# The inverse of the delta rule: its constant triangle as 128x128 block-diagonal tiles, one product for two heads

## The chip, the core and the metric

The kernel is one program on one core of a Trainium2 chip. The time is that of one execution on the device, in microseconds (us), and the number compared is the median of several executions. A core has TensorE (PE in the profile; its weight loads are listed apart as PEld), VectorE (DVE), ScalarE (ACT), GpSimd (POOL) and SyncE (SP), which issues most of the DMAs.

## What is computed

The reference is one decoder block on 512 tokens of width 1024, in float32: a projection, four DeltaNet heads (128 wide) beside four causal pooling groups, an output projection, and then a mixture of 32 experts, of which each token takes 4. The change touches one step of the DeltaNet heads, the inverse of a unit lower triangle of 64x64, one for each chunk of 64 tokens and each head (8 chunks x 4 heads = 32 triangles):

```python
a_mat = jnp.where(strict, jnp.einsum('bhnid,bhnjd->bhnij', k_beta, k) * decay, 0.0)
t_mat = lax.linalg.triangular_solve(a_mat, eye, left_side=True, lower=True, unit_diagonal=True)
u = jnp.einsum('bhnij,bhnjd->bhnid', t_mat, v * beta[..., None])
w = jnp.einsum('bhnij,bhnjd->bhnid', t_mat, k_beta * jnp.exp(g)[..., None])
```

The experts stream some 384 MB of weights (32 experts of 12 MB), and everything ahead of them works on 512 tokens.

## The kernel before

**Storage.** The two heads of a pair lie one above the other: head 0 of the pair on partitions 0 to 63, head 1 on 64 to 127. So the 32 triangles are 16 columns of tiles (NC = 16), each [128, 64] with two triangles in it. They are worked on in two groups of eight columns, a = 0 and a = 1. AT holds the constant triangles, TR the inverse so far (times -1 and turned, as the algorithm has it), TM its transpose, YM the masked product. All four lie in the large tile `ring`, or in `cat`, which later hold expert weights and activations.

**The inverse.** It is built in five levels (s = 0 to 4), which double the size of the blocks already inverted. For each level and group, PE makes the product of AT with TM (`level_products(s, a)`, into PSUM bank 2 + 2a), DVE masks it into YM (`level`, line 1032), PE makes the product of YM with TR (`level_update(s, a)`), ACT copies it back with its sign changed (`keep_inverse`, line 684), and DVE turns it (`turned`, line 922). Both products go through `tiles`: for each of the 8 columns one matmul for each head of the pair, with weights of 64 rows by 64 columns and 64 moving columns. A float32 matmul of the code stands as two MATMULs and two LDWEIGHTS in the trace, so that one call of `tiles` is 32 of each. There are ten calls of `level_products` and ten of `level_update`.

**The order on PE** is written out by hand: half of an input projection (`project(m, lo, hi)`, line 1468: 4 matmuls of 128x128 weights by 512 columns, 8 in the trace), then `level_products(s, 0)` and `level_update(s - 1, 1)`; the other half, then `level_products(s, 1)` and `level_update(s, 0)`. The first call, `level_products(0, 0)`, stands alone between two halves, and so does the last update. Nine groups hold one product and one update in a row.

**Around it.** DVE builds AT (lines 1019 and 1021) and the first TR (line 1023), turns it (line 922) and goes on to `conv(8)` (line 936), the causal convolution of a projection; PE's `project(m)` waits until `conv(m - 2)` has read its bank. POOL converts biases (lines 530, 533), then waits for lines 539 to 543, which spread decays over the chunks. SP loads `w_in` in ten pieces, and one 1 MB unit of the first expert's weights into slot 0 of the ring (`load_unit(0, 0, 0)`), behind the router's weights and ahead of the wait for the first projection. Later it loads `w_out` (line 384) after `u_ps`, the count of the products that use the finished inverse. The expert loop starts at about 307 us of the profile.

Of the kernel before, what the change touches and what calls it, by code (L numbers as in the profile page):

```python
# [25 lines left out]
CH = 64  # L26
NCH = T // CH
NC = 2 * NCH
# [16 lines left out]
UNIT = 2 * D  # L45
# [8 lines left out]
def moe_block(nc, x, attn_norm_w, w_in, conv_w, a_log, dt_bias, dn_norm_w, pool_w, pool_scale, w_out,  # L54
# [3 lines left out]
    with ctx:  # L58
        def sb(name, shape, dt=F32):
            return ctx.enter_context(nc.sbuf_tensor(name, shape, dt))  # L60

        def sem(name):
            return ctx.enter_context(nc.semaphore(name))


        ring = sb("ring", [P, RING * UNIT])
        late = ring[:, EARLY * UNIT:]

        def room(at, *dims):
            n = 1  # L70
            for d in dims:
                n *= d
            flat = late[:, at:at + n]
            if len(dims) == 2:
                return flat.rearrange("p (a b) -> p a b", a=dims[0])
            if len(dims) == 3:
                return flat.rearrange("p (a b c) -> p a b c", a=dims[0], b=dims[1])
            return flat
# [8 lines left out]
        junk = room(14400, D)  # L87
        GUM, NG, BI, AT, TM, YM = [room(14336 + 1024 * i, NC, CH) for i in range(6)]
        KKD, TRv = YM, YM
        sqq = room(20480, H, T)  # L90
        VTOK = room(20480, NC, P)
        wout = room(14336, KD, D)
# [130 lines left out]
        def bank(b, a=None):  # L223
            v = ps[:, b, :]
            return v.rearrange("p (a b) -> p a b", a=a) if a else v
# [9 lines left out]
        def bc(v, n, at):  # L235
# [20 lines left out]
        dx_ok, dexp_ok, nk_ok, rt_ok, rr_ok, ktok_ok, tr0_ok, tm_ok = [sem(n) for n in (  # L256
            "dx_ok", "dexp_ok", "nk_ok", "rt_ok", "rr_ok", "ktok_ok", "tr0_ok", "tm_ok")]
        qkt_ok, sqq_ok, nq_ok, vtok_ok, y_ps, ym_ok, tr_ps, tr_ok, trkv_ok = [sem(n) for n in (
            "qkt_ok", "sqq_ok", "nq_ok", "vtok_ok", "y_ps", "ym_ok", "tr_ps", "tr_ok", "trkv_ok")]
# [22 lines left out]
        def chain(eng, s, start=0):  # L282

            n = [0]

            def link(ins):
                n[0] += 1
                ins.then_inc(s, 1)
                eng.wait_ge(s, start + n[0])
            link.n = n  # L290
            return link

        def unit_src(e, u):

            if u < NGU:
                return w_gate_up[0, bass.ds(e, 1), u * P:(u + 1) * P, :].rearrange("a p c -> (a p) c")
            c = 2 * (u - NGU)
            return w_down[0, bass.ds(e, 1), c * P:(c + 2) * P, :].rearrange("a (c p) n -> p (a c) n", c=2)

        def unit_dst(slot, u):  # L300
            v = ring[:, slot * UNIT:(slot + 1) * UNIT]
            return v if u < NGU else v.rearrange("p (c n) -> p c n", c=2)
# [21 lines left out]
        def tap_of(m):  # L324

            return m + H if m < H else (m - H if m < 2 * H else m)
# [5 lines left out]
        def group(a):  # L332
            return slice(NC // 2 * a, NC // 2 * (a + 1))
# [11 lines left out]
        def _(sp):  # L345
# [20 lines left out]
            def load_unit(e, u, slot):  # L366
                sp.dma_start(unit_dst(slot, u), unit_src(e, u)).then_inc(slot_in[slot], 16)  # L367

            load_unit(0, 0, 0)
            sp.wait_ge(proj_ps, 2)  # L370
            load_piece(3)
            sp.wait_ge(bias_ok, 1)
# [9 lines left out]
                                 bc(zeros, TOPK, 1)).then_inc(zeroed, 16)  # L382
            sp.wait_ge(u_ps, 2)
            sp.dma_start(wout[:, :, :], w_out[0].rearrange("(k p) c -> p k c", p=P)).then_inc(wout_in, 16)
            sp.wait_ge(proj_ps, 18)
            load_unit(0, 8, 8)
            sp.wait_ge(pool_mix, 4)
# [85 lines left out]
        def _(pool):  # L473
            G = nc.gpsimd
            link = chain(pool, pool_step)
# [17 lines left out]
            for c in range(2):  # L493
                r = slice(CH * c, CH * (c + 1))
# [8 lines left out]
            for q in range(Q):  # L503
                r = slice(SLOTS * q, SLOTS * (q + 1))
# [24 lines left out]
            for n in range(3):  # L529
# [4 lines left out]
                else:  # L534
                    ins.then_inc(bias_ok, 1)

            pool.wait_ge(lvl_ok, 1)
            pool.wait_ge(g_ok, 1)
            G.tensor_tensor(GUM, mask(cz, NC), colb(gt[:, 8], CH), ALU.mult).then_inc(spread_ok, 1)
# [6 lines left out]
            for g, w in enumerate(WINDOWS):  # L546
                pool.wait_ge(silu_ok, NQKV + g + 1)
                src, s, i = pbuf[:, g], 1, 0
                while s < w:
                    dst = pool_t[:, i % 2]  # L550
                    link(G.tensor_tensor(dst[:, PAD:], src[:, PAD:], src[:, PAD - s:PAD + T - s], ALU.add))
                    src, s, i = dst, 2 * s, i + 1
# [316 lines left out]
        def _(dve):  # L869
            V = nc.vector  # L870
            link = chain(dve, dve_step)
# [48 lines left out]
            def turned(a):  # L920

                V.transpose(TM[:, group(a)].rearrange("p c f -> p (c f)"),
                            TR[:, group(a)].rearrange("p c f -> p (c f)")).then_inc(tm_ok, 1)
# [6 lines left out]
            def conv(m):  # L930

                t, n = cbuf[m % 2], tap_of(m)
                dve.wait_ge(tap_ok, m + 1)
                for j in range(1, CONV):
                    at = NCV + (n_conv - j) * NQKV + n
                    ins = V.scalar_tensor_tensor(out=t[:, j:], in0=bank(m % 2)[:, 0:T - j], scalar=pcol[:, at:at + 1],
                                                 in1=t[:, j:], op0=ALU.mult, op1=ALU.add)
                    if j < n_conv:
                        link(ins)
                    else:  # L940
                        ins.then_inc(conv_ok, 1)

            dve.wait_ge(bc_in, 48)
            for hh in range(2):
                r = slice(CH * hh, CH * (hh + 1))
# [40 lines left out]
            for hh in range(2):  # L986
                r = slice(CH * hh, CH * (hh + 1))
# [36 lines left out]
            for a in range(2):  # L1024
                dve.wait_ge(tr0_ok, a + 1)
                turned(a)
            conv(8)

            def level(s, a):
# [396 lines left out]
        def _(pe):  # L1426
            mm, tr = nc.tensor.matmul, nc.tensor.transpose
            def x_transposed(b, k, to):

                return tr(bank(to)[:, b * P:(b + 1) * P], xs[:, b, k * P:(k + 1) * P], ident)  # L1430

            pe.wait_ge(const_ok, 3)
            for b in range(TB):
                pe.wait_ge(x_in[b], 16)
                for k in range(KD - 1):
                    last = x_transposed(b, k, k)
# [7 lines left out]
            for b in range(TB):  # L1444
                pe.wait_ge(xdiag_ok, b + 1)
                last = mm(bank(7)[:, b * P:(b + 1) * P], ones, xdiag[:, b, :], start=True, stop=True)
# [53 lines left out]
            def rows(hh):  # L1500
                return slice(CH * hh, CH * (hh + 1))

            def chunk_of(v, n, h):
                return v[:, h, CH * n:CH * (n + 1)]
# [20 lines left out]
            def tiles(b, lhsT, rhs, a):  # L1525

                for c in range(NC // 2):
                    for hh in range(2):
                        last = mm(bank(b, 8)[rows(hh), c], lhsT[rows(hh), NC // 2 * a + c, :], rhs(hh, NC // 2 * a + c),  # L1529
                                  start=True, stop=True)  # L1530
                return last

            def of(v):
                return lambda hh, c: v[rows(hh), c, :]

            def level_products(s, a):

                pe.wait_ge(tm_ok, 2 * s + a + 1)
                tiles(2 + 2 * a, AT, of(TM), a).then_inc(y_ps, 1)

            def level_update(s, a):

                pe.wait_ge(ym_ok, 2 * s + a + 1)
                tiles(3 + 2 * a, YM, of(TR), a).then_inc(tr_ps, 1)
# [145 lines left out]
            for n in range(NCH):  # L1690
                for hh in range(2):
                    last = mm(ps[rows(hh), 7, 4 * n:4 * n + 4], ba_part[:, CH * n:CH * (n + 1)], S4[:, hh:2 * H:2],
                              start=True, stop=True)
# [4 lines left out]
            for i, c in enumerate((causal, same, first, second)):  # L1698
                last = mm(ps[:, 7, 64 + i * NC:64 + (i + 1) * NC], c, gt[:, 8], start=True, stop=True)
# [3 lines left out]
            for a in range(2):  # L1703
                last = mm(bank(2 + a, 8), same, GUM[:, group(a)], start=True, stop=True)
# [10 lines left out]
            for a in range(2):  # L1715
                last = mm(bank(2 + a, 8), later, BI[:, group(a)], start=True, stop=True)
# [7 lines left out]
            products(6, qs, prep_ps)  # L1724
            project(10, 0, 4)
            level_products(0, 0)
            project(10, 4)
            level_products(0, 1)
            level_update(0, 0)
            project(11, 0, 4)  # L1730
            level_products(1, 0)
            level_update(0, 1)
            project(11, 4)
# [4 lines left out]
            for n in range(NCH):  # L1738
                for hp in range(2):
                    for hh in range(2):  # L1740
                        c = 2 * n + hp
                        last = mm(ps[rows(hh), 6, c:c + 1], chunk_of(sqq, n, 2 * hp + hh), ones[:, 0:1], start=True, stop=True)
# [246 lines left out]
            for k in range(TOPK):  # L1989
                for half in range(2):  # L1990
                    mm(ps[:, 4 + half, :], ident_late, pairs_in[:, TB - 1, bass.ds(k * D + half * 512, 512)], start=k == 0,
                       stop=False)
            pe.wait_ge(x_in[TB - 1], 32)
            for half in range(2):
                last = mm(ps[:, 4 + half, :], ident_late, xs[:, TB - 1, bass.ds(half * 512, 512)], start=False, stop=True)
# [27 lines left out]
```

## Time and profile before

| what | value |
|---|---|
| median of 3 runs | 1320.4 us (1319.56 to 1321.78) |
| the profiled execution's own time | 1322.16 us |
| its span, first to last instruction | 1318.7 us |
| outside the span | 3.5 us |
| PE busy | 1269.6 us, 96% of the span |
| PEld busy | 747.0 us, 57% |
| DVE busy | 516.4 us, 39% |
| ACT and POOL busy | 190.9 and 160.8 us |
| granted TensorE clock, mean | 0.989 of full |

Busy time of PE is the time in which a matmul was under way; matmuls overlap, and their ends are modelled. So the price of a kind of matmul is read from the distance between starts, which the chain of waits also gives, and not from the mean duration of one. Idle time of an engine costs something only if the engine is on the chain that ends last.

### The profile page before, as it was taken

How to read it: one execution, taken by the hardware profiler on the slowest of the kernel's cores; microseconds unless marked ns; L12 is line 12 of the kernel's file. 1: busy time of each engine (PE TensorE's matmuls, PEld its weight loads, DVE VectorE, ACT ScalarE, POOL GpSimd, SP SyncE). 2: the span in 40 equal slices, each digit the busy share in tenths (PEclk: the TensorE clock that was granted, in tenths of full speed). 3: DMA queues.
4: the chain of work that ended last, by engine and by line, in shares of the span. 5: the costliest groups of instructions: out<-in, count | busy, mean ns of one | idle time of the engine just before them, and what ended most of it. 6: DMA issues, size and time to landing. Idle time of an engine off the chain costs nothing.

```text
span 1318.7 us, 52719 instructions
## 1 busy us (share of the span) xinstructions
PE 1269.6 (96%) x21836; PEld 747.0 (57%) x21837; DVE 516.4 (39%) x1734; ACT 190.9 (14%) x439; POOL 160.8 (12%) x267
## 2 busy tenths in 40 slices
PE   8999999999999999999999999999999999998896
PEld 4545655445565655666566656656656655654453
DVE  6554223347343333333333333433433433422237
ACT  3431123332000000000000000000000000000002
POOL 4100430122101011011011011010110110100010
PEclk9999999999999999999999999999999999999989
DMA  7453131509999999999999999999999999999997
GB/s 234 141 186 126 33 129 50 221 33 360 402 415 409 416 405 417 410 416 415 417 409 417 417 417 410 418 411 418 412 412 414 416 416 411 416 417 419 417 421 302
DMA packets 96888, 455.73 MB, mean 346 GB/s; under 512 B 11057, under 2 KB 23018, under 8 KB 63498
## 3 DMA queue, kind: packets, MB, share of 16 engines
q1 hardware_dynamic: 92784, 445.69, 83.9%
q0 software_dynamic: 3888, 8.40, 1.7%
q8 instruction: 86, 1.41, 0.4%
q14 instruction: 24, 0.20, 0.0%
q10 hardware_dynamic: 106, 0.04, 0.0%
HBM read 432.53 MB, written 23.27 MB: 346 GB/s over the span
## 4 chain that ended last, share of the span: by engine, by line
DMA 52%; PE 43%; DVE 2%; issue 2%; SPq 1%; POOL 0%; DVEq 0%; ACT 0%; POOLq 0%; ACTq 0%
DMA ring<-in_w_gate_up_dram 32%; DMA ring<-in_w_down_dram 19%; PE ps L1892 12%; PE ps L1468 11%; PE ps L1944 5%; PE ps L1488 4%; PE ps L1858 2%; PE ps L1529 2%; PE ps L1522 1%; PE ps L1924 1%; PE ps L1430 0%; PE ps L1884 0%; SPq L367 0%; DVE ring L1421 0%; PE ps L1614 0%
## 5 line engine op out<-in xcount | busy, mean ns | idle before, releaser
L1892 PE MATMUL ps<-ring,cat 128*32 128x256 f32 x9856 | 554.8, 382 | 7.8 <-DMA ring<-in_w_gate_up_dram 7.8
L1892 PEld LDWEIGHTS ps<-ring,cat 128*32 128x32 f32 x9856 | 305.4, 111 | 226.6 <-DMA ring<-in_w_gate_up_dram 10.7
L1944 PE MATMUL ps<-ring,cat 128*32 128x256 f32 x4800 | 278.1, 381 | 15.9 <-DMA ring<-in_w_down_dram 15.8
L1944 PEld LDWEIGHTS ps<-ring,cat 128*32 128x32 f32 x4800 | 142.3, 110 | 122.6 <-DMA ring<-in_w_down_dram 20.9
L1468 PE MATMUL ps<-hbuf,ring 128*128 128x512 f32 x320 | 147.7, 608 | 1.7 <-DVE hbuf L917 1.7
L1262 DVE TENSOR_REDUCE wslot<-ps 128x2 f32<-128x6 f32 x75 | 12.3, 164 | 323.2 <-ACT cat L843 321.6
L596 POOL DMA_INDIRECT pair_rows_dram<-cat,rowi x73 | 72.7, 996 | 451.6 <-ACT cat L843 451.6
L835 ACT ACTIVATE cat<-cat 128x128 f32<-128x128 f32 x154 | 47.7, 310 | 528.9 <-DVE cat L1286 528.9
L1858 PE MATMUL ps<-hbuf,cat 128*32 128x256 bf16 x2432 | 104.7, 273 | 1.5 <-DVE cat L1386 1.5
L1468 PEld LDWEIGHTS ps<-hbuf,ring 128*128 128x128 f32 x320 | 58.9, 192 | 68.3 <-issue 66.6
L1286 DVE TENSOR_SCALAR cat<-ps 128x128 f32<-128x128 f32 x154 | 44.8, 291 | 134.5 <-PE ps L1892 134.3
L843 ACT ACTIVATE cat<-ps,wslot 128x256 f32<-128x256 f32 x75 | 35.5, 474 | 371.4 <-PE ps L1944 371.4
L1858 PE MATMUL ps<-aux,cat 128*32 128x256 bf16 x1216 | 86.8, 273 | 0.0
L1858 PEld LDWEIGHTS ps<-hbuf,cat 128*32 128x32 bf16 x2432 | 66.5, 97 | 17.5 <-DVE cat L1386 2.0
L592 POOL TENSOR_TENSOR rowi<-rowj,qcol 128x1 int32<-128x1 int32 x75 | 15.2, 202 | 416.4 <-DMA pair_rows_dram<-cat,rowi 387.6
L1381 DVE COPY selu<-E 96x32 bf16 x75 | 13.3, 177 | 124.5 <-issue 124.5
L1488 PE MATMUL ps<-ring,cat 128*128 128x512 f32 x128 | 58.5, 601 | 2.3 <-DVE ring L1177 1.4
L1386 DVE TENSOR_TENSOR cat<-iotaf,rank 128x512 bf16 x75 | 51.9, 692 | 12.0 <-DVE gie L1382 12.0
L1294 DVE STREAM_TRANSPOSE cat<-cat 128x128 f32<-128x128 f32 x154 | 48.0, 312 | 5.3
L1290 DVE SCALAR_TENSOR_TENSOR cat<-cat 128x128 f32<-128x128 f32 x154 | 45.0, 292 | 5.3
L1293 DVE TENSOR_TENSOR cat<-cat 128x128 f32<-128x128 f32 x154 | 45.0, 292 | 5.2
L1287 DVE TENSOR_SCALAR cat<-ps 128x128 f32<-128x128 f32 x154 | 43.2, 280 | 0.0
(363 smaller groups left out, 816.9 us busy)
## 6 DMA issues: line engine op xcount, KB each, us to landing
ring<-in_w_gate_up_dram SPq DMA_DIRECT2D x256, 1024.0 KB, 10.0
ring<-in_w_down_dram SPq DMA_DIRECT2D x128, 1024.0 KB, 10.2
ring<-in_w_in_dram SPq DMA_DIRECT2D x10, 1024.0 KB, 6.3
pair_rows_dram<-cat SPq DMA_DIRECT2D x4, 2048.0 KB, 10.9
ring<-pair_rows_dram SPq DMA_DIRECT2D x4, 2048.0 KB, 18.3
ring<-in_w_out_dram SPq DMA_DIRECT2D x1, 4096.0 KB, 12.7
ring<-in_x_dram SPq DMA_DIRECT2D x4, 512.0 KB, 5.3
x_rows_dram<-ring SPq DMA_DIRECT2D x2, 1024.0 KB, 10.5
```

Of the source, the lines that this page charges most:

```text
L596: G.indirect_dma_start(out=into, out_offset=bass.IndirectOffsetOnAxis(ap=rowi[:, 0:1], axis=0), in_=ys, in_offset=None, bounds_check=limit ...
L835: A(sg[:, half], gc[:, half], ACT.Sigmoid, scale=ALPHA).then_inc(sg_ok, 1)
L1286: V.tensor_scalar(gc[:, half], ps[:, b, 0:P], LIMIT, None, ALU.min).then_inc(gc_ok, 1)
L1290: step(V.scalar_tensor_tensor(out=uc[:, half], in0=uc[:, half], scalar=1.0, in1=gc[:, half], op0=ALU.add, op1=ALU.mult), uc_step, n * 2 + 2)
L1293: step(V.tensor_tensor(act_[:, half], uc[:, half], sg[:, half], ALU.mult), act_ok, n + 1)
L1294: V.transpose(to[:, half], act_[:, half]).then_inc(told, by)
L1386: step(V.tensor_tensor(hot[:, :, :, :], slots, mine, ALU.is_equal), hot_ok, count)
L1468: last = mm(bank(m % 2), win[:, piece % 3, k, m % 2 * P:(m % 2 + 1) * P], hT[:, k, :], start=k == 0, stop=k == KD - 1)
L1488: last = mm(bank(n % 2), catT[:, k, b * P:(b + 1) * P], wout[:, k, 512 * half:512 * (half + 1)], start=i == 0, stop=i == KD - 1)
L1858: last = mm(ps[SLOTS * q:SLOTS * (q + 1), 2, 0:QD].rearrange("p (j i) -> p j i", i=SLOTS), hot[:, b, 0, :], rows, start=b == 0 and n == 0, ...
L1892: last = mm(ps[SLOTS * q:SLOTS * (q + 1), banks[half], 0:2 * P].rearrange("p (s j i) -> p s j i", s=2, j=4), x[:, SLOTS * u:SLOTS * (u + 1 ...
L1944: last = mm(ps[SLOTS * q:SLOTS * (q + 1), 1, 0:QD], actT[:, c // 4, SLOTS * (c % 4):SLOTS * (c % 4 + 1)], w[:, i, q * QD:(q + 1) * QD], st ...
```

## The change

The triangles AT are written a second time into a new tile ATd, of 16 tiles of [128, 128], each with the two heads' triangles on its diagonal and zeros elsewhere. `level_products` then makes one matmul for each column of tiles, with 128x128 weights from ATd and all 128 partitions of TM as the moving operand, 64 columns, by the new function `joined`. `level_update` still goes through `tiles`. ATd lies in slot 0 of the ring, so the load of the first expert's unit 0 into that slot is issued after the wait for `u_ps`, behind the load of `w_out`. POOL clears ATd after the biases; DVE fills the diagonal blocks with four copies of [64, 8 x 64], between the turning of the first TR and `conv(8)`.

```diff
+        ATd = ring[:, 0:UNIT].rearrange("p (c f) -> p c f", c=NC)
...
-            load_unit(0, 0, 0)
             sp.wait_ge(proj_ps, 2)
             load_piece(3)
...
             sp.wait_ge(u_ps, 2)
             sp.dma_start(wout[:, :, :], w_out[0].rearrange("(k p) c -> p k c", p=P)).then_inc(wout_in, 16)
+            load_unit(0, 0, 0)
             sp.wait_ge(proj_ps, 18)
             load_unit(0, 8, 8)
...
+            link(G.memset(ATd, 0.0))
             pool.wait_ge(lvl_ok, 1)
             pool.wait_ge(g_ok, 1)
...
             for a in range(2):
                 dve.wait_ge(tr0_ok, a + 1)
                 turned(a)
+            for a in range(2):
+                for hh in range(2):
+                    r = slice(CH * hh, CH * (hh + 1))
+                    V.tensor_copy(ATd[r, group(a), r], AT[r, group(a), :]).then_inc(tr0_ok, 1)
             conv(8)
...
+            def joined(b, lhsT, rhs, a):
+
+                for c in range(NC // 2):
+                    last = mm(bank(b, 8)[:, c], lhsT[:, NC // 2 * a + c, :], rhs[:, NC // 2 * a + c, :], start=True, stop=True)
+                return last
...
             def level_products(s, a):
 
                 pe.wait_ge(tm_ok, 2 * s + a + 1)
-                tiles(2 + 2 * a, AT, of(TM), a).then_inc(y_ps, 1)
+                if s == 0:
+                    pe.wait_ge(tr0_ok, 2 * a + 4)
+                joined(2 + 2 * a, ATd, TM, a).then_inc(y_ps, 1)
```

## Rows read from the trace of the kernel before

**Rows 1.** The page: busy time by engine, and the DMA line of the 40 slices.

```profile
PE 1269.6 (96%) x21836; PEld 747.0 (57%) x21837; DVE 516.4 (39%) x1734; ACT 190.9 (14%) x439; POOL 160.8 (12%) x267
...
DMA  7453131509999999999999999999999999999997
```

**Rows 2.** Chain that ended last, in order of time: start us, us, what.

```profile
82.88 13.93 PE ps L1468 x32
...
98.82 3.63 PE ps L1468 x8
102.45 1.08 PE ps L1529 x32
...
107.16 2.01 PE ps L1529 x64
...
122.42 5.33 PE ps L1468 x8
```

**Rows 3.** The same chain at other shapes of weights.

```profile
44.88 0.80 PE ps L1699 x8
...
120.46 1.96 PE ps L1742 x64
...
172.00 1.93 PE ps L1566 x32
...
232.46 0.89 PE ps L1638 x8
```

**Rows 4.** Groups by line and shape, to 330 us: xcount, busy us, mean ns.

```profile
L1566 PE MATMUL ps<-cat,ring 64*128 64x64 f32 x64 | 4.0, 275 | 0.0
...
L1638 PE MATMUL ps<-ring 128*128 128x128 f32 x32 | 4.3, 278 | 0.0
...
L1742 PE MATMUL ps<-ring 128*64 128x1 f32 x64 | 2.0, 198 | 0.0
...
L1699 PE MATMUL ps<-ring 128*128 128x16 f32 x8 | 1.0, 252 | 0.0
```

**Rows 5.** The weight loads of the same window, by line and shape.

```profile
L1529 PEld LDWEIGHTS ps<-ring 64*64 64x64 f32 x320 | 10.1, 135 | 7.6 <-issue 7.6
...
L1699 PEld LDWEIGHTS ps<-ring 128*128 128x128 f32 x8 | 1.1, 192 | 0.5 <-issue 0.5
```

**Rows 6.** Timeline of DVE, 76 to 124 us: start us, us.

```profile
88.14 1.30 DVE L922 STREAM_TRANSPOSE ring<-cat 128x512 f32<-128x512 f32 x2
90.70 2.31 DVE L936 SCALAR_TENSOR_TENSOR ring<-ps,pcol,ring 128x511 f32<-128x511 f32 x3 [1.26 <-ACT ring L654]
```

**Rows 7.** DVE by line and shape: a copy of 512 columns.

```profile
L1184 DVE COPY ring<-ps 128x512 f32<-128x512 f32 x8 | 5.2, 687 | 8.1 <-PE ps L1650 8.1
```

**Rows 8.** POOL: the timeline around the clearing, and a clearing by shape.

```profile
41.80 1.90 POOL L539 TENSOR_TENSOR ring<-aux,ring 128x1024 f32<-128x1024 f32 x1 [15.44 <-DVE ring L981]
...
L526 POOL MEMSET cat<- 128x1024 f32 x1 | 1.0, 951 | 0.1
```

**Rows 9.** PE's first projection, SP's DMA issues, and PE's first use of w_out.

```profile
13.45 3.67 PE L1468 MATMUL ps<-hbuf,ring 128*128 128x512 f32 x8 [1.66 <-DVE hbuf L917]
...
16.25 2.28 SPq L367 DMA_DIRECT2D ring<-in_w_gate_up_dram  x1
...
179.50 0.37 SPq L384 DMA_DIRECT2D ring<-in_w_out_dram  x1
...
ring<-in_w_out_dram SPq DMA_DIRECT2D x1, 4096.0 KB, 12.7
...
226.98 1.96 PE L1488 MATMUL ps<-ring,cat 128*128 128x512 f32 x4 [0.89 <-issue]
...
296.87 1.45 SPq L367 DMA_DIRECT2D ring<-in_w_down_dram  x3
```

**Rows 10.** Windows: PE, PEld, DVE, ACT, POOL busy, granted clock, DMA share, GB/s.

```profile
124.40:125.40 1.00, 1.00 (x2) 0.33 (x1) 0.00 (x0) 0.31 (x1) 0.00 (x0) 0.50 0.00 0
...
170.05:173.90 3.85, 3.85 (x66) 3.61 (x65) 0.00 (x0) 1.68 (x3) 2.86 (x3) 1.00 0.01 4
```

## The prediction

> **What bounds the kernel now.** I read the page first [rows 1]. PE is busy for 96% of the span, but that number covers two kinds of time. The line of the DMA engines is low in the first nine of the 40 slices (33 us each) and at 9 tenths after that: up to about 297 us the DMAs hardly matter, and from there on the experts' weights set the pace. So the second view is the chain of waits, cut at the place of the change. From 82.88 us on it holds PE's groups end to end with nothing between them [rows 2], and the windows at the other end of the stage give PE as busy for the whole of their length, such as 3.85 of 3.85 us from 170.05 [rows 10]. Whatever a group of matmuls takes there, the stage takes. Of the expert stage the reader is to see only that the DMA line stays at 9 [rows 1]: the stream of weights, once started, has a rate of its own, and it starts with the issues at 296.87 us, which wait for the output projection [rows 9]. A delay of PE ahead of that point therefore moves the start of the stream, and the stream can't win it back, since its bytes are the same and the slice just before, 264 to 297 us, stands at 0 [rows 1].
>
> **What the change removes.** Ten calls of `tiles` leave `level_products`. A half projection takes 3.63 us between two groups of small tiles, a lone call 1.08 us, and two calls in a row 2.01 us [rows 2]. In the long row without small tiles beside it, 32 matmuls of the projection take 13.93 us, so eight take 3.48 [rows 2]; the 0.15 us that 3.63 has above it is the passage from small tiles to large weights and back. I put one call of 32 matmuls at 0.98 us (half of 2.01, less its share of the passage), 31 ns for each. The form stands 320 times under this name, ten calls of 32 [rows 5].
>
> **What it adds on PE.** A call of `joined` has 8 matmuls of the code, 16 in the trace, with weights of 128x128 and 64 moving columns. No row of before has that shape, so I bound the distance between two of them. With 128x128 weights and only 16 moving columns, eight take 0.80 us, 100 ns each; with 128x128 weights and 128 moving columns, eight take 0.89 us, 111 ns each [rows 3, 4]. Eight times as many moving columns cost 11% more: what is paid for is not the moving columns but the loading of the weights. The loads say the same: one of 128x128 lasts 192 ns where one of 64x64 lasts 135 [rows 5]. I read this so: the two 64x64 loads of a pair of heads go to different rows and columns of the array and run beside each other, and two of 128x128 can't. Then 32 small ones at 31 ns each stand against 16 large ones at about 108. The row with 64 rows by 128 columns and 64 moving columns, where neighbours still alternate between the two halves of the rows, costs 1.93 us for 32, 60 ns each [rows 3, 4]; it is the floor for the new shape. Being nearest to the two 128x128 rows, which lie on both sides of 64 moving columns, I take 108 ns: 16 x 0.108 = 1.73 us for a call.
>
> The sum: nine calls stand beside an update, 1.73 - 0.98 = +0.75 us each, +6.75. The passage isn't saved there, because the update's small tiles still stand between large weights. The first call stands alone: half a projection and that call take 3.63 + 1.08 = 4.71 us now [rows 2], and 3.48 + 1.73 = 5.21 then, +0.50, since both passages go. Together +7.25 us. From 100 and 111 ns the same sum gives 6.0 and 7.7 us.
>
> The Trainium skill has a rule that would make the change pay nothing or even a little ("TensorE: Matmul & The Clock Gate", Back-to-back issue gap): warm matmuls follow each other at their moving columns divided by 2.4 GHz, plus 2.5 ns. By it a float32 matmul of two passes over 64 columns would come every 56 ns, a call would take 0.9 us and the ten calls would save 0.8 us. The row with 16 moving columns, 100 ns apart, speaks against it. Another section there, on LDWEIGHTS, has the load depend on its columns alone, which is what the rows show.
>
> **What it adds elsewhere, at no cost in time.** On DVE, four copies stand between the second transpose, which ends at 89.44 us, and `conv(8)`, which starts at 90.70 after 1.26 us of waiting for ACT [rows 6]. A copy of 512 columns took 687 ns out of PSUM [rows 7]; from one SBUF place to another it may take less. Four cost at most 2.75 us, so `conv(8)` starts at most 1.5 us later and ends at 94.5 in place of 93.0 us; PE needs its result only at the projection that starts at 98.82, and ATd itself at 102.45 [rows 2]. Without that cover it would cost those 1.5 us once. On POOL, the clearing covers 2048 columns; 1024 took 951 ns, so 1.9 us, in a wait of 15.44 us [rows 8]. On SP one issue moves. At its old place nothing waits for it, since it is the last issue before SP's wait for the projection: PE's wait of 1.66 us at the start is over at 13.45 us [rows 9], and the chain behind it has no DMA in it. Behind `w_out` at 179.50 it adds 1 MB to 4 MB that took 12.7 us; even at a quarter more, 15.9 us, `w_out` is there at 195.4, and PE wants it first at 226.98 [rows 9]. Unit 0 itself is wanted by the expert loop, after 297 us. What SP has behind it is a wait for the eighteenth projection, which comes long after one more issue. The new wait of PE for the copies can't bite, by the same 10 us. DVE gets each product 0.75 us later, and has over 3 us, half a projection, before the update of the same group.
>
> The last pieces, the lone updates and everything behind them to 297 us follow PE, so they move with it. Together: 1322.2 + 7.2 = 1329.4 us for the profiled execution, with a span of 1325.9. The median of the runs lay 1.8 us below the profiled execution, so for it 1320.4 + 7.2 = 1327.6 us.
>
> **The rivals.** (a) Moving columns set the price, 56 to 60 ns: a call takes 0.90 to 0.96 us, and with 0.93 the sum is 9 x -0.05 and, for the lone call, 3.48 + 0.93 - 4.71 = -0.30, together -0.8 us. The time would be 1319.6 us, no change that can be told. For it speaks only the row at 60 ns with alternating row halves. (b) The other side: the price is one per instruction. The matmuls with one moving column and weights of 128x64 come every 31 ns (1.96 us for 64 [rows 3, 4]), just as those of 64 columns and 64x64 do. If that held at 128x128, a call would take 0.5 us, and the ten would save 9 x 0.48 and 0.73 = 5.0 us: 1315.4 us, faster. A gain begins where 16 matmuls take less than 0.98 us, below 61 ns, and can be told from no change below some 47; the row at 100 ns is against it. (c) Loads and matmuls don't overlap: 108 ns and 54 (the projection's 435 ns for 512 columns, an eighth of it), 2.6 us a call, 9 x 1.6 + 1.4 = +16 us, 1336 us. The row with 128 moving columns, at 111 ns, would have to be at over 200. (d) The granted clock. It stands at 0.50, the 1.2 GHz level, at 124.4 us, after 2 us of matmuls that move one column each [rows 3, 4, 10]; the projection that it hits takes 5.33 us in place of 3.48 [rows 2], 1.85 us lost. The new calls move 64 columns in 108 ns, fewer for the time than now, so another fall is possible: one gives 1329.4 us, two 1331.3. Against it, 3.85 us of small products at 170.05 us passed at full clock [rows 10]. (e) PE's delay is absorbed later, as part of some wait: 1320.4 to 1324. I see no such wait, since PE's first is at 226.98 us, 0.89 us long, and comes from PE's own work through ACT.
>
> The Trainium skill's "TensorEngine Tiling (Array Packing)", Key Properties, says that a change of tiling mode drains the engine. The change doesn't alter the number of such passages in the nine groups and takes two away at the lone call; by the rows these are worth 0.15 to 0.25 us, which is in the sum.
>
> **How the numbers follow.** Chances: my forecast 0.79, (a) 0.05, (b) 0.02, (c) 0.03, (d) 0.08, (e) 0.03. The forecast's own range is 1326.4 to 1328.1 by the two bounds, 100 and 111 ns, and about 1 us more on either side, since the three runs of before lay up to 0.8 us below and 1.4 above their median. For the lower end I add the floor's side, part of (e), and for the upper one (d) and the 1.85 us of a clock that falls in some executions and not in others: 1324.6 to 1331.4. 0.2%, about what a measurement of this kernel can tell from no change, is 2.6 us. Slower by more: the forecast, (c), (d) and part of (e), 0.92. Within: (a) and the rest of (e), 0.06. Faster: (b), 0.02.
>
> **What the profile of the changed kernel would show.** A form of 128x128 weights with 64 moving columns, 160 matmuls, whose loads last 190 ns; in the chain 16 of them in 1.6 to 1.8 us where 32 took 1; groups of project, joined and tiles of 6.4 us in place of 5.64; the first w_out matmul near 234 us in place of 226.98; the burst of loads at 304 in place of 296.87; the expert stage unchanged in length. DVE's `conv(8)` may start 1.5 us later with nothing behind it. The prediction is wrong if the 16 take under 1 us, or over 2.2, if PE has a new wait of its own in the level stage, or if the expert stage gets shorter by what the first stage lost.

## The result, and the profile after

The changed kernel took 1330.26 us (median of 4 runs, 1329.33 to 1331.56), the kernel before beside it 1319.98 us: a ratio of 1.0071, 95% interval 1.0057 to 1.0085, so +9.4 us with 7.5 to 11.2 by the interval, and +10.3 by the medians. The forecast was 1327.6 us, +7.2. The time lies in the range and below its upper end by 1.1 us. Of all executions reported below one was slow, of the kernel with only the load moved (1641.57 us at a granted clock of 0.753), and its ratio leaves it out.

The profiled execution has a span of 1329.8 us, 11.1 more than before. The chain of waits of the new kernel, in order of time, shows how the level stage begins; its lines answer to [rows 2]:

```profile
84.83 13.93 PE ps L1474 x32
...
100.78 3.63 PE ps L1474 x8
104.41 1.73 PE ps L1542 x16
106.14 3.49 PE ps L1474 x8
109.62 1.73 PE ps L1542 x16
111.36 1.08 PE ps L1535 x32
112.43 3.63 PE ps L1474 x8
116.06 1.73 PE ps L1542 x16
...
127.33 5.23 PE ps L1474 x8
```

L1542 is `joined`, L1535 `tiles`, L1474 the projection. The reader is to see three things: the new product takes 1.73 us for 16 matmuls, the group of project, joined and tiles 6.44 us in place of 5.64, and the update beside it 1.08. The groups by line and shape give the form, with the loads below it:

```profile
L1542 PE MATMUL ps<-ring 128*128 128x64 f32 x160 | 18.9, 272 | 0.0
L1535 PE MATMUL ps<-cat,ring 64*64 64x64 f32 x320 | 11.5, 221 | 0.0
...
L1542 PEld LDWEIGHTS ps<-ring 128*128 128x128 f32 x160 | 19.4, 192 | 4.8 <-issue 4.8
L1535 PEld LDWEIGHTS ps<-cat,ring 64*64 64x64 f32 x320 | 10.1, 134 | 1.4 <-issue 0.8
```

A load of 128x128 lasts 192 ns, as it did under other lines [rows 5]; successive ones are 1.73 / 16 = 108 ns apart. So the records of neighbouring loads overlap here too, and the price is the distance, not the duration.

DVE, POOL and SP in the same profile, for the steps that were to cost nothing (timelines of the three; the one row of w_out is PE's):

```profile
90.09 1.30 DVE L924 STREAM_TRANSPOSE ring<-cat 128x512 f32<-128x512 f32 x2
91.31 1.74 DVE L1032 COPY ring<-ring 64x512 f32<-64x512 f32 x4
93.08 2.31 DVE L938 SCALAR_TENSOR_TENSOR ring<-ps,pcol,ring 128x511 f32<-128x511 f32 x3
...
26.62 1.80 POOL L538 MEMSET ring<- 128x2048 f32 x1
44.40 1.90 POOL L541 TENSOR_TENSOR ring<-aux,ring 128x1024 f32<-128x1024 f32 x1 [15.98 <-DVE ring L983]
...
189.09 0.37 SPq L384 DMA_DIRECT2D ring<-in_w_out_dram  x1
189.50 0.58 SPq L368 DMA_DIRECT2D ring<-in_w_gate_up_dram  x1
...
236.57 1.95 PE L1494 MATMUL ps<-ring,cat 128*128 128x512 f32 x4 [0.89 <-issue]
...
306.46 1.45 SPq L368 DMA_DIRECT2D ring<-in_w_down_dram  x3
```

Before PE's first matmul of w_out stands the same 0.89 us of wait as in [rows 9], and it comes 9.59 us later, as does the burst of loads (306.46 against 296.87).

So the 11.1 us of the two spans part in this way. The long row of 32 projection matmuls ahead of the inverse begins at 84.83 in place of 82.88: +1.95 ahead of the change. From there to the first matmul of w_out it is 151.74 us in place of 144.10: +7.64, the level stage. From w_out to the burst there is no difference. From the burst to the end it is 1023.3 in place of 1021.8: +1.5. The forecast had only the middle one. The experiments had two questions: whether the price of the weight loads is the cause of the middle term, and what the other two are.

### The profile page after: what moved, and what is told of

Its sections match the earlier page's. It is cut to its first block, busy times and chain, and to the rows that moved or that the text cites. A ratio compares the mean times of both kernels' runs of the same rounds, so it can differ in the third digit from the quotient of the medians.

```text
span 1329.8 us, 52407 instructions
## 1 busy us (share of the span) xinstructions
PE 1274.9 (96%) x21677; PEld 758.2 (57%) x21677; DVE 523.3 (39%) x1738; ACT 191.0 (14%) x439; POOL 164.5 (12%) x268
## 4 chain that ended last, share of the span: by engine, by line
PE 54%; DMA 42%; DVE 2%; issue 1%; SPq 0%; DVEq 0%; ACT 0%; POOL 0%; POOLq 0%; ACTq 0%
DMA ring<-in_w_gate_up_dram 23%; PE ps L1906 19%; DMA ring<-in_w_down_dram 16%; PE ps L1474 11%; PE ps L1958 8%; PE ps L1494 4%; PE ps L1872 3%; PE ps L1542 1%; DMA x_rows_dram<-cat,rowi 1%; PE ps L1535 1%; PE ps L1898 1%; PE ps L1528 1%; DMA ring<-in_x_dram 1%; PE ps L1938 1%; PE ps L1949 0%
## 5 line engine op out<-in xcount | busy, mean ns | idle before, releaser
L1474 PE MATMUL ps<-hbuf,ring 128*128 128x512 f32 x320 | 149.3, 613 | 1.7 <-DVE hbuf L919 1.7
L1474 PEld LDWEIGHTS ps<-hbuf,ring 128*128 128x128 f32 x320 | 59.5, 194 | 69.2 <-issue 66.8
L594 POOL TENSOR_TENSOR rowi<-rowj,qcol 128x1 int32<-128x1 int32 x75 | 15.9, 212 | 416.3 <-DMA pair_rows_dram<-cat,rowi 387.8
## 6 DMA issues: line engine op xcount, KB each, us to landing
ring<-in_w_out_dram SPq DMA_DIRECT2D x1, 4096.0 KB, 12.9
```

The source lines that it names most:

```text
L1474: last = mm(bank(m % 2), win[:, piece % 3, k, m % 2 * P:(m % 2 + 1) * P], hT[:, k, :], start=k == 0, stop=k == KD - 1)
```

## The experiments

In each I read the same stretch of the profile, from the row of 32 projection matmuls to the first matmul of w_out, and call it the level stage; the clock falls in some executions within it, which costs 1.6 to 1.7 us (5.33 us for a half projection in [rows 2], where without a fall it has 3.63, so 1.70; the prediction took 1.85 from the wrong base of 3.48). "Before" is the kernel before, run beside the others on the same chip.

### The load of unit 0 moved, and nothing else

```diff
-            load_unit(0, 0, 0)
             sp.wait_ge(proj_ps, 2)
...
             sp.dma_start(wout[:, :, :], w_out[0].rearrange("(k p) c -> p k c", p=P)).then_inc(wout_in, 16)
+            load_unit(0, 0, 0)
```

> The kernel before with one thing changed: unit 0 of the first expert is loaded behind w_out. The changed kernel is 10.3 us slower, and its profile shows only 7.64 us of that in the level stage. Theory A (the rest is chance: a clock fall near 15 us in one execution, time outside the span, the rate of the weight stream): 0 us, within 1 us of before. Rival B (the moved load costs the rest): +2 to +3 us, and the profile shows where, either at the start, or behind w_out, or as a longer expert stage.

1321.44 us against 1320.58; ratio 1.0007 (0.9998 to 1.0016). Its level stage is 225.01 - 82.60 = 142.41 us without a clock fall; before's 144.10, less the 1.70 of its fall, is 142.40. A second time, with an interval of its own:

> The kernel before with the load of unit 0 moved, once more. The first time the ratio was 1.0007 with an interval that reached 1. Theory A (chance): 1.000 within 0.0007, and the profile of this execution differs from the last by its clock falls alone. Rival B: 1.0007 or more again, about 1 us.

Ratio 1.0000 (0.9991 to 1.0010). Rival B asked for 2 to 3 us; neither ratio has it, though the first interval reaches 2.1 us. A cost of up to 1.3 us stays within both intervals.

### All of the change but the product

```diff
-                joined(2 + 2 * a, ATd, TM, a).then_inc(y_ps, 1)
+                tiles(2 + 2 * a, AT, of(TM), a).then_inc(y_ps, 1)
```

> All of the change but the product itself: ATd is cleared and filled and the load is moved, and level_products still goes through tiles of AT. Theory A: 0 us, PE's groups of 5.64 us as before, conv(8) about 0.4 us later with nothing behind it. Rival B (the moved load): +2 to +3. Rival C (the copies and the clearing cost something by way of DVE or POOL): slower than the kernel with only the load moved by 1 us or more.

Ratio 1.0010 (1.0001 to 1.0019), 1.3 us with an interval from 0.1 to 2.5; level stage 142.41 us. Then the same with ATd where `zs` lies later and the load at the start, which leaves the clearing and the copies alone:

> ATd cleared and filled in the place of zs, the load at the start, the product through tiles of AT: the clearing and the copies alone. PE's level stage is 142.3 us without clock falls in every kernel with tiles. Theory A (the two cost nothing): within 0.07% of before. Rival C (they cost the 1 us or so that the kernels with ATd seem to have beyond the level stage): 1.0007 to 1.0015.

Ratio 1.0004 (0.9994 to 1.0013), level stage 225.35 - 82.95 = 142.40 us. The clearing and the four copies cost nothing that can be told, and the level stage lies between 142.40 and 142.42 us in all five profiles with tiles. Without `joined` no version loses more than 1.3 us by its ratio, and the upper ends of the intervals are 1.3 to 2.5 us; only the interval of the kernel with all but the product leaves out 0, by 0.1 us.

### The product with the load left at the start

```diff
-        ATd = ring[:, 0:UNIT].rearrange("p (c f) -> p c f", c=NC)
+        ATd = room(6144, NC, P)
...
+            load_unit(0, 0, 0)
             sp.wait_ge(proj_ps, 2)
```

> The changed kernel with ATd in the place of zs, which isn't written before the levels are over, so that unit 0 is loaded at the start as before. Theory A: as slow as the changed kernel, +7.5 to +10 us to before, the level stage longer by 7.6. Rival B: 2 to 3 us less than the changed kernel.

> The changed kernel once more, five rounds beside before on the chip of the other three. If the 2.7 us beyond the level stage are chance, the difference is nearer to 7.6 than to 10.3 us, or the spans without a clock fall at the start differ by some 8 us. If they belong to the change, it is again 10 us, and the profile has an expert stage about 1.5 us longer.

| kernel | first time | second time |
|---|---|---|
| joined, load at the start | 1.0067 (1.0053 to 1.0081) | 1.0059 (1.0046 to 1.0072) |
| the changed kernel beside it | 1.0082 (1.0069 to 1.0096) | 1.0067 (1.0054 to 1.0080) |

> The new product with ATd in the place of zs and the load at the start, once more. The level stage is 7.7 us longer. Theory A: 1.0058 to 1.0067 to before. If it is as slow as the changed kernel beside it, the place of the load is cleared; if it is 1.5 us or more faster, the moved load costs that.

> The changed kernel a third time, beside the one with the other place. Theory A: equal to it within 1 us. Rival B (the moved load): slower by 1.5 us or more, as the first pair was (8.8 and 10.8 us over before).

With the load at the start the level stage is 233.10 - 83.00 = 150.10 us the first time and 233.09 - 82.99 = 150.10 the second: 7.7 us over the 142.4 of the kernels with tiles. The four ratios, of 1320.6 and 1321.2 us, come to 8.8 and 7.8 us for it and to 10.8 and 8.8 for the changed kernel. So the new product alone accounts for 7.7 us by the profile and about 8.3 by the timed runs. The changed kernel is 2.0 us above it in the first pair and 1.0 in the second, with intervals that overlap; the expectations had asked for 1.5 us or more if the moved load costs something and for less than 1 if not, so the pairs don't decide it.

### The start: a clock fall that comes ahead of what was moved

The changed kernel's profile has this near its start, in the chain:

```profile
13.71 5.37 PE ps L1474 x8
```

and before has 3.67 us for the same eight matmuls [rows 9]. The 1.70 us are a fall of the granted clock to the 1.2 GHz level, from about 14.4 us on (columns as in [rows 10]):

```profile
14.00:15.00 1.00, 1.00 (x3) 0.36 (x2) 1.00 (x3) 0.00 (x0) 0.00 (x0) 0.72 1.01 217
15.00:16.00 1.00, 1.00 (x3) 0.48 (x2) 1.00 (x2) 0.00 (x0) 0.00 (x0) 0.50 0.73 169
```

Windows ahead of it, in the changed kernel, in the one with the load at the start, and in the changed kernel's third run (PE, PEld, DVE, ACT, POOL busy, granted clock, DMA share, GB/s):

```profile
8.90:12.30 3.40, 2.34 (x16) 1.90 (x16) 1.39 (x6) 1.87 (x6) 2.77 (x11) 1.00 1.15 338
```

```profile
8.90:12.30 3.40, 2.50 (x19) 1.88 (x17) 1.58 (x6) 1.82 (x6) 2.77 (x11) 1.00 1.15 337
```

```profile
8.90:12.30 3.40, 2.21 (x16) 1.83 (x16) 1.95 (x7) 1.35 (x3) 2.77 (x11) 1.00 1.15 332
```

The first has the fall behind it; the second and the third haven't. A fall at this place stood in the profiles of the changed kernel and of its second run, in that with all but the product, and in the second run of the one with only the load moved, and in none of the other nine. All four are among the six profiles in which the load of unit 0 is moved; of the seven with the load at its place none has it. The traces show no way from one to the other: the issue that the change takes away stood at 16.25 us in the trace of before, and the fall begins at 14.4. And two kernels with the load moved, the changed one and the one with only that, were profiled with the fall and without. So 1.7 of the 1.95 us are this fall, which comes in some executions and not in others; whether the moved load makes it more frequent, 13 profiles don't show. PE's busy time just before doesn't settle it: it was 2.34 us with the fall and 2.21 in the third row without.

### What is paid for: the weight load

> ATd in the place of zs and the load at the start, and each of the 8 products of a call split by columns of its weights: two matmuls with weights of 128x64, one for each head's 64 output rows, all 128 partitions of TM moving. 32 matmuls a call again. Theory A (the width of a weight load sets the price, and two loads of 64 columns run beside each other): 31 ns each, 1.0 us a call, groups of 5.64 us, the time of before, within 0.1%. Rival D (reading all 128 rows or the zeros of the block diagonal costs the time): 1.7 us or more a call, +7 us. If the helpers' cost is that of the moved load, this kernel, which doesn't move it, has none of it.

```diff
             def joined(b, lhsT, rhs, a):
                 for c in range(NC // 2):
-                    last = mm(bank(b, 8)[:, c], lhsT[:, NC // 2 * a + c, :], rhs[:, NC // 2 * a + c, :], start=True, stop=True)
+                    for hh in range(2):
+                        last = mm(bank(b, 8)[rows(hh), c], lhsT[:, NC // 2 * a + c, rows(hh)], rhs[:, NC // 2 * a + c, :],
+                                  start=True, stop=True)
```

Its chain of waits (L1543 is the split product, L1535 the update by tiles):

```profile
102.76 1.08 PE ps L1543 x32
103.84 3.63 PE ps L1474 x8
107.47 1.08 PE ps L1543 x32
108.55 1.08 PE ps L1535 x32
109.63 3.63 PE ps L1474 x8
```

The same block-diagonal data, the same 128 rows with the same zeros and the same 64 moving columns, but loads of 64 columns: 1.08 us a call, the price of `tiles`, and not 1.73. Rival D is out. The level stage bears it out: 228.60 - 83.18 = 145.42 us, less 1.67 for its clock fall, is 143.75, 1.35 over the 142.40 with tiles. The trace of before had this shape already, and beside it the same weights with twice the moving columns:

```profile
96.81 2.02 PE ps L1512 x64
...
135.40 1.90 PE ps L1522 x32
```

```profile
L1522 PE MATMUL ps<-ring 128*64 128x128 f32 x128 | 7.9, 276 | 0.0
L1512 PE MATMUL ps<-ring 128*64 128x64 f32 x128 | 4.2, 224 | 0.0
```

64 moving columns cost 2.02 / 64 = 32 ns, 128 cost 1.90 / 32 = 59 ns. So with weights of 64 columns the moving columns do count at 128. But the group isn't 5.64 us, as I had written, but 3.63 + 1.08 + 1.08 = 5.79, and nine groups make +1.35 us. Two calls of `tiles` in a row take 2.01 us [rows 2], and here a call with weights of 128x64 and one of 64x64 take 2.16: there is a passage of 0.15 us between the two shapes. The ratio was 1.0022 (1.0009 to 1.0035), 2.9 us with 1.2 to 4.6, above the 0.1% that I had given; the 1.35 lie in the interval.

> ATd in the place of zs; each product of a call split by its moving columns, twice 32 in place of 64, with the same 128x128 weights loaded for each. Theory A (price per weight load, 108 ns): 32 x 0.108 = 3.46 us a call, the groups at 8.2 us, +7.65 + 10 x 1.73 = +25 us to before. Rival E (moving columns set the price, 64 of them in 108 ns): 1.73 us a call as with the changed kernel, +8 to +9 us. Rival F (load and matmul one behind the other, about 81 and 27 ns for 32 columns): between, 2.6 to 2.8 us a call.

```diff
-                    last = mm(bank(b, 8)[:, c], lhsT[:, NC // 2 * a + c, :], rhs[:, NC // 2 * a + c, :], start=True, stop=True)
+                    for i in range(2):
+                        last = mm(bank(b, 8)[:, c, 32 * i:32 * i + 32], lhsT[:, NC // 2 * a + c, :],
+                                  rhs[:, NC // 2 * a + c, 32 * i:32 * i + 32], start=True, stop=True)
```

Its chain:

```profile
102.53 3.49 PE ps L1543 x32
106.02 5.21 PE ps L1474 x8
111.24 3.49 PE ps L1543 x32
...
122.93 1.51 PE ps L1535 x32
```

As many moving columns as in the changed kernel and twice the loads: 3.49 us a call, 109 ns each, twice the price. With 32 columns or with 64, the distance is the same to 1 or 2 ns. That is Theory A, 3.49 us for 3.46; a price by moving columns (E) and one of load plus matmul (F) are both out. What isn't parted is the load from its own matmul: every matmul here has a load of its own, and no run uses one load for two. The runs show the price of the pair, and that it goes by the columns of the weights. The Trainium skill ("TensorE: Matmul & The Clock Gate", LDWEIGHTS) gives a load as its columns divided by 1.2 GHz, whatever its rows, which for 128 is 106.7 ns; the trace agrees with 108 to 110. The rule of the Trainium skill that was weighed in the prediction ("TensorE: Matmul & The Clock Gate", Back-to-back issue gap) would by the same working, an estimate, give 29 ns for two passes over 32 columns and 0.93 us a call. The Trainium skill says in that section that this gap is too low at few columns, since it leaves out the weight load, which the prediction didn't tell.

The kernel took 1353.14 us, ratio 1.0243, +32 us, where I had expected +25. The lines above show why: 5.21 us for the projection in place of 3.49, and 1.51 for an update in place of 1.08. Its profile has four clock falls in the level stage, as these windows show (clock before the DMA share):

```profile
104.20:107.60 3.40, 3.40 (x20) 2.58 (x20) 0.69 (x1) 0.00 (x0) 0.00 (x0) 0.81 0.93 381
121.30:124.70 3.40, 3.40 (x48) 3.24 (x48) 0.69 (x1) 0.21 (x1) 0.00 (x0) 0.80 0.00 0
148.60:152.00 3.40, 3.40 (x35) 3.34 (x36) 0.52 (x1) 0.00 (x0) 3.23 (x3) 0.80 0.00 0
169.10:172.50 3.40, 3.40 (x49) 3.24 (x48) 0.69 (x1) 0.00 (x0) 3.15 (x4) 0.80 0.85 288
```

Its level stage is 257.07 - 82.96 = 174.11 us, and the stage without falls would be 142.4 + 7.7 + 10 x (3.49 - 1.73) = 167.7: 6.4 us for four falls. PE is busy in all four windows; what it did shortly before each was a call of matmuls of 32 columns, 109 ns apart. The first comes 0.3 us behind the end of the stage's first such call (the clock is at 1.00 up to 106.0 us and has fallen by 106.4). That is rival (d) of the prediction, at half the moving columns of the change. The changed kernel's profiles have no fall in the level stage beyond the one that before has too.

### Twice the delay

```diff
-                joined(2 + 2 * a, ATd, TM, a).then_inc(y_ps, 1)
+                joined(2 + 2 * a, ATd, TM, a)
+                joined(2 + 2 * a, ATd, TM, a).then_inc(y_ps, 1)
```

> ATd in the place of zs; each call of joined made twice, the second over the first. Theory A: each further call is 1.73 us in a stage in which PE is never idle, and all of it reaches the end: +17.3 us to the kernel with ATd in that place, +26 to before. If part of PE's delay is absorbed by the weight stream, it is less than 15 us; if a longer level stage also lengthens the expert stage (the 1 to 3 us that the level stage doesn't explain), it is 20 or more.

The chain and SP's issues of its profile:

```profile
103.67 3.52 PE ps L1542 x32
107.19 3.49 PE ps L1474 x8
110.68 3.52 PE ps L1542 x32
...
321.96 1.45 SPq L368 DMA_DIRECT2D ring<-in_w_down_dram  x3
```

Two calls take 3.52 us, 110 ns a matmul. The level stage is 252.06 - 84.10 = 167.96 us, 17.9 over the kernel with one. By the ratios, 1.0212 (1.0193 to 1.0230) less 1.0067 or 1.0059, the whole is 19 to 20 us, with some 3 either way. So PE's delay passes to the end, one for one within that. And the stage from the burst to the end is 1345.0 - 321.96 = 1023.0 us, no longer than the 1024.4 and 1023.1 of the two profiles with one call and ATd in the same place, so that the expert stage doesn't grow with the delay ahead of it.

## Why the prediction was right

The mechanism and its sum held; the whole did so with some luck. The forecast of +7.2 us lies a little below the measured interval of 7.5 to 11.2. The range held the result because it had been widened by a clock fall, and in the profiled pair 1.7 us were such a fall, but at the start and not in the level stage, where the prediction looked for it.

**The price of the new product** was the step that mattered, and it held: 108 ns by two rows on either side of it, 108 in the profile, 109 and 110 in two variants. That half the instructions cost more is a matter of the width of the weights: the split in columns brings the price back to 1.08 us with the same data. That two narrow loads run beside each other in the array and two wide ones can't is my reading of these prices and isn't shown; the records of two wide loads overlap as well, 192 ns long and 108 apart. The row at 111 ns was a weaker bound than I took it for: 128 moving columns are a quarter of the projection's 435 ns, 109 ns, so that they alone could set it. The row at 100 ns and the split in moving columns don't have this doubt.

**The call that went away was over-priced.** I put `tiles` at 0.98 us and said that no passage changes in the nine groups. The trace says it otherwise: a second call of the same shape adds 2.01 - 1.08 = 0.93, and the 0.15 of the passage comes with the change of shape. Old group: 3.48 + 2 x 0.93 + 0.30 = 5.64; new: 3.48 + 1.73 + 0.93 + 0.30 = 6.44. That is +0.80 each, +7.2, and +0.51 for the first call, whose neighbouring projection falls from 3.63 to 3.49 us while the one ahead of it stays at 3.63, since other small tiles precede it. Sum 7.7, measured 7.64 in the profiled pair, with a fall in the same place in both (1.70 and 1.60 us), and 7.7 by the stages without falls. I had 7.25. As for the number of passages, the old groups had two and the new ones too; my sum counted a part of one as the price of the call.

**The steps at no cost** held. The copies took 1.74 us for four, 435 ns each where I had bounded them by 687, and `conv(8)` began 0.4 us later relative to PE's projections (93.08 - 1.95 = 91.13 against 90.70). The clearing took 1.80 us for 1.9 expected, in the wait ahead of line 541. `w_out` landed in 12.9 us where it had taken 12.7, with 5 MB under way where I had allowed 15.9.

**The rivals.** (a), (b) and (c) fell by the 108 ns and by the two splits. (e) fell by the doubled kernel. (d), a further fall in the level stage, came in no profile of the changed kernel, but did in the variant with 32 columns. What I had left out is that a fall may also stand at the start: it took 1.7 us of the profiled 11.1.

**What stays open.** The runs put the changed kernel at 9.4, 10.8 and 8.8 us over before, the level stage explains 7.7, and the other place of ATd gave 8.8 and 7.8. Some 1 to 1.5 us therefore go with the changed place of the load, or with falls at the start, which would account for 1.1 us if they came in four executions of six as in the profiles; the kernel with only the load moved, at 0.9 and 0.0 us by its ratios, speaks against the whole of it. Some 0.6 us more go with neither. In single profiles the time from the burst to the end ran from 1021.1 to 1024.6 us: the five with tiles have 1021.1 to 1023.8, mean 1022.4, the five with one call of `joined` 1023.0 to 1024.6, mean 1023.7. The two kinds overlap, and the doubled kernel's 1023.0 doesn't go on in that direction. The intervals, 0.1% and more either way, don't tell such differences apart, and no mechanism was found for them.

## What to carry to other kernels

Price small float32 matmuls of up to 64 moving columns by the width of their weights and not by their number or their moving columns: here 128 columns of weights on 128 rows cost 108 ns each, and 64 columns, alternating between two parts of the array, 29 to 32. At 128 moving columns this ends: the weights of 64 columns cost 59 ns there. A block-diagonal weight that joins two 64x64 products halves the instructions and takes 1.73 us where the row of small ones took 0.93. And when a call is taken out of a row of like calls, price it by the step from one to two of them (2.01 - 1.08), since the passage between shapes stays behind.

## What the runs showed that I had not expected

- A passage of 0.15 us stands also between weights of 128x64 and of 64x64, both small: 1.08 + 1.08 us in a row where two of one shape take 2.01.
- Matmuls of 32 moving columns, 109 ns apart, in calls of 3.49 us let the granted clock fall four times in the level stage at a cost of about 1.6 us each, while PE counts as busy throughout; with 64 columns at the same distance, in the doubled kernel's calls of 3.52 us, there is no fall in that stage. That is one profile of each.
- A copy of 64 partitions by 512 columns within SBUF took 435 ns, against 687 for 128 partitions out of PSUM [rows 7].
